# Prompt rows as a fifth tile of the compression pairs, gates evacuated in place, spatial steps spread over the pairs

## The reference, cut to what matters

```python
h = rmsnorm(x, lw['norm_g'])
proj = h @ lw['w_in']                       # q, k_cmp, v_cmp, k_sel, ..., za, u, v, zb, r
...
def compress(rows, params):                 # windows of 32 rows, one every 16
    w1, b1, w2, b2 = params
    ...
    blocks = rows[:, idx].transpose(0, 1, 3, 2, 4).reshape(B, n_cmp, G, CMP_BLOCK * dh)
    return jax.nn.gelu(blocks @ w1 + b1) @ w2 + b2
...
    kc = compress(jnp.concatenate([gather_pages(ck_cmp), k_cmp], axis=1), lw['cmp_k'])   # decode, 63 windows
    kc = compress(k_cmp, lw['cmp_k'])                                                    # prompt, 31 windows
...
v_n = layernorm(jax.nn.gelu(v), lw['v_norm_g'], lw['v_norm_b'])
sgu = jax.nn.gelu(u) * spatial_gate(v_n, lw['w_spatial'], lw['b_spatial'])
pb = (sgu * jax.nn.silu(zb)) @ lw['w_pb']
```

## Time and profile before

| | us |
|---|---|
| median of 3 runs | 543.88 |
| lowest and highest | 541.86, 543.99 |
| the profiled execution, its own time | 543.01 |
| its span in the trace | 541.3 |
| PE busy | 523.7 (97%) |
| DVE busy | 331.2 (61%) |
| ACT busy | 243.1 (45%) |
| POOL busy | 157.0 (29%) |

### The profile page before, as it was taken

One profiled execution on the slowest core, in us unless ns is written; L12 is line 12 of the kernel. 1 busy time (PEld: TensorE's weight loads), 2 busy tenths in 40 slices (PEclk: granted clock), 3 DMA queues, 4 the chain that ended last, 5 costly groups with the idle time before them and its releaser, 6 DMA issues.

```text
span 541.3 us, 12831 instructions
## 1 busy us (share of the span) xinstructions
PE 523.7 (97%) x5198; PEld 473.3 (87%) x5198; DVE 331.2 (61%) x838; ACT 243.1 (45%) x564; POOL 157.0 (29%) x257
## 2 busy tenths in 40 slices
PE   6899999999999999999989999999999999999995
PEld 4899999999999998987978766767779999999995
DVE  4723231388898765674564678687753477763565
ACT  6543424534533323241241887677674432323334
POOL 0006933044414633734000066473453000000000
PEclk9999999999999999999999999999999999999998
DMA  8527652448525465877331267563454435306104
GB/s 296 214 82 218 235 181 80 154 141 290 173 61 195 142 198 168 264 282 238 101 97 40 79 155 186 148 155 100 128 140 125 131 114 155 119 1 196 40 7 161
DMA packets 59789, 81.05 MB, mean 150 GB/s; under 512 B 7825, under 2 KB 49233, under 8 KB 59218
## 3 DMA queue, kind: packets, MB, share of 16 engines
q1 hardware_dynamic: 48320, 49.97, 30.4%
q0 software_dynamic: 10688, 29.14, 17.6%
q10 hardware_dynamic: 722, 1.12, 0.6%
HBM read 65.23 MB, written 8.13 MB: 136 GB/s over the span
## 4 chain that ended last, share of the span: by engine, by line
PE 91%; DVE 3%; issue 2%; ACT 1%; DMA 1%; POOL 1%; DVEq 0%
PE m L1729 62%; PE so L2028 4%; PE so L2037 3%; PE so L1900 3%; PE so L1903 3%; PE so L1901 3%; PE m L1813 2%; PE so L1939 2%; PE so L1877 1%; PE so L1988 1%; DMA U<-p_turn 1%; PE t L1865 1%; POOL U L1002 1%; PE t L1755 1%; PE so L1742 1%
## 5 line engine op out<-in xcount | busy, mean ns | idle before, releaser
L1729 PE MATMUL m<-h_hi,w_hi 128*128 128x272 f32 x448 | 132.7, 296 | 1.0 <-DVE za L1426 0.8
L1729 PE MATMUL m<-h_hi,w_lo 128*128 128x272 f32 x448 | 129.2, 288 | 0.0
L1729 PE MATMUL m<-h_lo,w_hi 128*128 128x272 f32 x448 | 128.7, 287 | 0.0
L1729 PE MATMUL m<-w_hi,h_hi 128*128 128x256 f32 (+2 forms) x360 | 104.1, 289 | 2.4 <-issue 1.9
L1729 PE MATMUL m<-w_hi,h_lo 128*128 128x256 f32 (+2 forms) x360 | 101.9, 283 | 0.0
L1729 PE MATMUL m<-w_lo,h_hi 128*128 128x256 f32 (+2 forms) x360 | 101.9, 283 | 0.0
L1313 DVE TENSOR_TENSOR w_lo<-raw,w_hi 128x1024 fp32r<-128x1024 f32 (+2 forms) x62 | 71.0, 1155 | 42.6 <-ACT w_hi L1046 42.5
L1729 PEld LDWEIGHTS m<-h_hi,w_hi 128*128 128x128 f32 x448 | 84.3, 188 | 13.4 <-issue 10.2
L1002 POOL DMA_DIRECT2D U<-p_turn x108 | 58.2, 547 | 104.0 <-DVE p_turn L1635 102.6
L1729 PEld LDWEIGHTS m<-h_hi,w_lo 128*128 128x128 f32 x448 | 84.5, 189 | 0.0
L1729 PEld LDWEIGHTS m<-h_lo,w_hi 128*128 128x128 f32 x448 | 84.4, 188 | 0.0
(11 more groups left out here) (301 smaller groups left out, 904.3 us busy)
## 6 DMA issues: line engine op xcount, KB each, us to landing
raw<-in_w_in SPq DMA_DIRECT2D x36, 512.0 KB
U<-in_x_p SPq DMA_DIRECT2D x8, 512.0 KB, 5.9
raw<-in_w_o SPq DMA_DIRECT2D x8, 512.0 KB
U<-p_turn POOLq DMA_DIRECT2D x54, 64.0 KB, 2.6
U<-p_turn SPq DMA_DIRECT2D x42, 64.0 KB, 2.8
raw<-in_w_in SPq DMA_DIRECT2D x8, 256.0 KB
raw<-in_w_pa SPq DMA_DIRECT2D x8, 256.0 KB
raw<-in_w_pb SPq DMA_DIRECT2D x4, 512.0 KB
```

The costliest lines, as they stand in the source:

```text
L1729: ins = mm(out, lhs(a, k), rhs(b, k), start=(k == 0 and a + b == 0), stop=(k == n - 1 and a == 1))
```

## The change

- The `hid` steps are gone. The prompt's turned rows are a fifth tile of pairs 1 and 6: five casts, five subtractions, and `hidh` and `hidl` of these two pairs have 320 columns in place of 256. The prompt's windows thereby take the split in three passes too. Its gelu is a second ScalarE instruction into `hid_rows`, and its `kc` matmuls stand among those of the pair.
- `xt_sb` grows to 5 tiles, and the second half of `w1_hi` moves to the columns that hold `kT`. `kT` is therefore written to DRAM at step `kTs` (`k_dram`, 512 KB), read back at step `kt 0 6`, and the prompt's first scores wait for it (`k_back`).
- The order: pair 1 starts one V block earlier, two V blocks stand between the pairs instead, all four turns of a pair stand ahead of what was between them, and the spatial steps stand with pair 6 (one), pair 7 (two) and pair 8 (two).
- All four U0 gates go straight into `sg` (`DIRECT`), so that two `mix` steps fall away, and a spatial step multiplies two groups into the gates.
- The squares of the decode rows are summed on VectorE with `tensor_tensor_reduce`.

```diff
-    u0 = [("main", SLOT["U0"], 1, hf) for hf in range(2)]
     u1 = [("main", SLOT["U1"], a, hf) for a in range(2) for hf in range(2)]
-    extra = {3: [("ln", NT), ("lnr",)], 6: [("sp", 2), ("sp", 3), ("ln2", 4)],
-             7: [("sp", 4), ("mix", u0[0]), ("mix", u0[1])], 8: [("mix", u1[0]), ("mix", u1[1])], 9: [("mix", u1[2])]}
+    norm = {4: 0, 6: 2, 7: 3, 8: 4}
+    extra = {3: [("ln", NT), ("lnr",)], 6: [("sp", 0)], 7: [("sp", 1), ("sp", 2)], 8: [("sp", 3), ("sp", 4)],
+             9: [("mix", x) for x in u1[:3]]}
...
+    def early(count):
+
+        n = len(order)
+        main(count)
+        order[n:] = [x for x in order[n:] if x not in (("ln", NT), ("lnr",))]
...
     order += [("w1hi", 0)]
     turn(5)
-    main(3)
-    order += [("hid", 0), ("w1lo", 0)]
+    main(2)
+    order += [("w1lo", 0)]
     for c in range(1, NCH):
         behind = [("hidl", c - 1)] if c - 1 in PAIRS else []
+        tiles = ([(c - 1, 0)] if c in WIDE_PAIRS else []) + [(c, n) for n in range(4)]
         if c == 5:
             order += behind
             turn(1)
-            order += [("sp", 0), ("w1hi", 1), ("ln2", 1), ("w1lo", 1)] + four("xh", 6) + [("hid", 5), ("kc", 4), ("sp", 1), ("ln2", 2)]
+            order += [("w1hi", 1), ("ln2", 1), ("w1lo", 1)] + [("xh", x, n) for x, n in [(5, 0)] + [(6, n) for n in range(4)]]
+            order += [("kc", 4)]
             main(1)
             continue
-        cast = four("xh", c) if c != 6 else []
+        cast = [("xh", *x) for x in tiles] if c != 6 else []
         order += cast[:2] + behind + cast[2:]
-        if c == 1:
-            main(1)
-        if c == 8:
-            order.append(u1[0])
+        if c in (2, 3):
+            early(1)
         s, after = take()
-        order += [("part", s, 0, KD)] + four("xl", c) + [("kc", c - 1), ("hidh", c)]
+        order += [("part", s, 0, KD)] + [("xl", *x) for x in tiles] + ([("kc", c - 1)] if c - 1 in PAIRS else []) + [("hidh", c)]
         turn(2)
-        if c in (4, 6):
-            order.append(("ln2", 0 if c == 4 else 3))
-        order += ([s] if c != 7 else []) + [x for x in after if x not in (("ln", NT), ("lnr",))] + extra.get(c, [])
+        if c in norm:
+            order.append(("ln2", norm[c]))
         turn(2)
+        order += [s] + after + extra.get(c, [])
     order += [("hidl", NCH - 1)]
...
-DIRECT = [("main", SLOT["U0"], 0, hf) for hf in range(2)]
+DIRECT = [("main", SLOT["U0"], a, hf) for a in range(2) for hf in range(2)]
...
-        w1_hi = [placed("w1_hi0", 3072, [P, 8, P], F32R), placed("w1_hi1", 5376 + 4104, [P, 8, P], F32R)]
+        w1_hi = [placed(f"w1_hi{n}", 3072 - 1024 * n, [P, 8, P], F32R) for n in range(2)]
         w1_lo = placed("w1_lo", 5376 + 11272, [P, 16, P], F32R)
-        xt_sb = placed("xt_sb", 5376, [P, 4100], F32R)
-        xt_hi, xt_lo = xt_sb[:, 0:2050], xt_sb[:, 2050:4100]
+        xt_sb = placed("xt_sb", 5376, [P, 5124], F32R)
+        xt_hi, xt_lo = xt_sb[:, 0:2562], xt_sb[:, 2562:5124]
...
+                elif s[0] == "kTs":
+                    for y in range(2):
+                        wait_evacuated(sp, T_AT[("kT", y)])
+                    sp.dma_start(k_dram, kT[:, :, :]).then_inc(k_saved, 16)
+                elif s == ("kt", 0, 6):
+                    sp.wait_ge(hid_sum, len(PAIRS))
+                    sp.dma_start(kT[:, :, :], k_dram).then_inc(k_back, 16)
...
-                    _, before, m = TURNS[t - RING]
-                    if before in PAIRS:
-                        pool.wait_ge(xt_lo_done, 4 * PAIRS.index(before) + m + 1)
-                    else:
-                        pool.wait_ge(hid_sum, before + 1)
+                    pool.wait_ge(xt_lo_done, LOW_AT[TURNS[t - RING][1:]] + 1)
...
+                    if i == NT:
+                        continue
...
-                        if s == DIRECT[0]:
-                            act.wait_ge(hid_sum, 1)
-                        nc.scalar.activation(sg[:, 0, s[3] * HALF:(s[3] + 1) * HALF], m[:, 0:HALF], ACT.Gelu_apprx_tanh).then_inc(main_act, 1)
+                        nc.scalar.activation(sg[:, s[2], s[3] * HALF:(s[3] + 1) * HALF], m[:, 0:HALF], ACT.Gelu_apprx_tanh).then_inc(main_act, 1)
...
+                        act.wait_ge(k_saved, 16)
...
+                    if c in WIDE_PAIRS:
+                        x = S[k % 2][:, 0:320].rearrange("p (g n) -> p g n", g=G)
+                        nc.scalar.activation(out, x[:, :, 0:P], ACT.Gelu_apprx_tanh, bias=b1)
+                        nc.scalar.activation(hid_rows.rearrange("p (g n) -> p g n", g=G)[:, :, 0:NCP], x[:, :, P:P + NCP],
+                                             ACT.Gelu_apprx_tanh, bias=b1).then_inc(hid_ready, 1)
+                    else:
+                        nc.scalar.activation(hid_at[k % 2], S[k % 2][:, 0:256], ACT.Gelu_apprx_tanh, bias=b1).then_inc(hid_ready, 1)
...
+                elif kind == "sq" and s[1] == NT:
+                    x = x_in[0:TS, NT, :]
+                    dve.wait_ge(x_loaded[NT], 16)
+                    v.tensor_tensor_reduce(U[0:TS, 10240:11264], x, x, 1.0, 0.0, ALU.mult, ALU.add, st[0:TS, NT:NT + 1]).then_inc(rows_squared, 1)
...
-                        dve.wait_ge(hid_sum, 1)
                         dve.wait_ge(kc_ready, 4)
                         for s0 in DIRECT:
                             wait_main_read(dve, s0)
                     else:
                         wait_evacuated(dve, T_AT[("sp", i - 1)])
-                        dve.wait_ge(kc_ready, 5)
                     if i < NT:
-                        v.tensor_tensor(sg[:, 1:4, tok(i)], tb[:, P:4 * P].rearrange("p (g n) -> p g n", g=3),
-                                        b_sp[:, P:4 * P].rearrange("p (g n) -> p g n", g=3), ALU.add)
-                        seq(v.tensor_tensor(sp_t[:, 0:r], tb[:, 0:r], b_sp[:, 0:r], ALU.add))
+                        t4, b4 = (x.rearrange("p (g n) -> p g n", g=4) for x in (tb[:, :], b_sp))
+                        v.tensor_tensor(sg[:, 2:4, tok(i)], t4[:, 2:4, :], b4[:, 2:4, :], ALU.add)
+                        seq(v.tensor_tensor(sp_t[:, :, :], t4[:, 0:2, :], b4[:, 0:2, :], ALU.add))
...
-                elif kind == "hid":
-                    c = s[1]
-                    k = TURN_AT[c, 0]
-                    pe.wait_ge(w1_loaded[c // 5], 16)
-                    pe.wait_ge(x_turned, k + 1)
-                    if c >= 2:
-                        pe.wait_ge(hid_ready, c - 1)
-                    x = ring[:, k % RING, :].rearrange("p (r g e m) -> p r e g m", r=4, g=G, e=2)
-                    for j in range(16):
-                        o, r, e = j // 8, j // 2 % 4, j % 2
-                        ins = mm(S[c % 2][:, 0:2 * NCP], w1_at[c // 5][:, j, :], x[:, r, e, :, o:o + NCP], start=(j == 0), stop=(j == 15))
-                    ins.then_inc(hid_sum, 1)
...
-                            return part[:, 512 * r + o:512 * r + o + 512].rearrange("p (g e n) -> p e g n", g=G, e=2)[:, e, :, :]
+                            return part[:, 640 * r + o:640 * r + o + 640].rearrange("p (g e n) -> p e g n", g=G, e=2)[:, e, :, 0:n]
...
+                            mm(out, w, x(xt_hi), start=(j == 0), stop=False, skip_group_check=True)
+                            ins = mm(out, w1_lo[:, j, :], x(xt_hi), start=False, stop=False, skip_group_check=True)
                         else:
-                            ins = mm(out[:, 0:256], w, x(xt_lo), start=False, stop=(j == 15), skip_group_check=True)
+                            ins = mm(out, w, x(xt_lo), start=False, stop=(j == 15), skip_group_check=True)
```

More of the change, by code:

```diff
@@ L154 @@
 PAIRS = [c for c in range(NCH) if c % 5]
+PAIR = {c: n for n, c in enumerate(PAIRS)}
+PAIR.update({c: PAIR[c + 1] for c in range(0, NCH, 5)})
+WIDE_PAIRS = [c + 1 for c in range(0, NCH, 5)]
 TILES = (3, 2, 1, 0)
@@ L468 @@
 TURN_AT = {s[1:]: n for n, s in enumerate(TURNS)}
+HIGH_AT = {s[1:]: n for n, s in enumerate(x for x in ORDER if x[0] == "xh")}
+LOW_AT = {s[1:]: n for n, s in enumerate(x for x in ORDER if x[0] == "xl")}
 NKEY = 3 * QB
@@ L993, in _ @@
                     load_upto(TURN_AT[s[1:]] + RING + 1)
[L994 to L998 removed]
+                elif s == ("sp", NT):
+                    wait_evacuated(pool, T_AT[s])
+                    pool.wait_ge(out_done, 16 * N_OUT)
+                    for k in range(7):
+                        load_key(0, k)
                 elif s[0] == "tt" and moves_with(s[1]) == s[1]:
@@ L2021, in _ @@
                         pe.wait_ge(s_exp, NQ)
+                        pe.wait_ge(k_back, 16)
                     for c in range(2):
```

137 lines of the change are left out of this document (67 added, 70 removed).

## The result

| | us |
|---|---|
| kernel before, median of 20 runs | 542.53 |
| kernel after, median of 20 runs | 544.03 |
| ratio after to before, 95% interval | 1.0025 (1.0013 to 1.0037) |
| profiled execution of after, its span | 544.36, 542.6 |

The change made the kernel a quarter of a per cent slower: by the medians 1.5 us, clear of noise but small. I had forecast 2.8 us faster, 540.6, with a range from 538.0 to 543.2; 544.03 lies outside it. The first part of the page (busy us, share, instructions) shows what was meant to happen: TensorE has 64 matmuls fewer than in the earlier trace rows and is busy 1.5 us less. The span is 1.3 us longer all the same.

What follows compares the result with a forecast made beforehand. TensorE, busy 97% of the span, was taken to bound the kernel; -4.2 us of matmuls, +2.2 of stalls and -0.8 at the start gave -2.8, so 540.6 us, range 538.0 to 543.2.

Steps and rivals of the forecast that it cites:

- start: Kernel start: with the decode rows' squares on VectorE, TensorE goes on sooner; -0.8 us, bounds 0 and -0.9.
- (a): Before the first `hidh`, where `hid` stood: TensorE waits for five casts on ScalarE; +0.45 us.
- the two `hid`: The two `hid` steps in the compression are removed from TensorE; -7.1 us.
- wide passes: Pairs 1 and 6: 96 matmuls grow from 256 to 320 columns; +2.9 us.
- prompt's `kc`: The prompt's `kc` matmuls only move into pairs 1 and 6; taken as 0.
- (b): `kc` of pair 4, directly behind `hidl`, waits for ScalarE's gelu; +0.8 us.
- (c): `hidh` of pair 4 waits for a late load, turn, `ln`, `lnr` and casts; +1.0 us, 0 to 3.0 by landing time.
- (d): Pair 7: copies of pair 8 meet its loads, so its casts come late; +0.2 us, 0 to 1.5.
- old stall of 0.23: The 0.23 us in which TensorE idles in the compression before the change goes away.
- My signs of being wrong: Landings of over 6 us in more than one pair, or wide matmuls at 0.13 us.
- "no gain": Rival: VectorE waits for landings in several pairs, (c) and (d) come to 4.5 us; 543.6 us, chance 0.20.
- "slower" rival: A circle of subtraction, load and turn closes from landings of 5.2 us, seven pairs lose 1.5 each; about 549.8, chance 0.05.

Runs made afterwards that it cites:

- experiment 11: Kernel of experiment 9 with the two wide passes back at 256 columns, so the compressed prompt rows are not computed: 535.15 us (0.9852).
- experiment 13: Changed kernel with its order kept, only SyncE's 16 window copies moved out of the compression to an earlier stretch: 539.84 us (0.9942).
- experiment 1: Changed kernel with the decode rows' statistics and square root (`ln`, `lnr`) moved ahead of the last two turns of pair 4: 539.03 us (0.993).
- Experiments 3: Changed kernel with 20 useless matmuls of 128x256 filling TensorE's wait before `kc` 3: 542.67 us (1.0002).
- experiment 14: The changed kernel as it is, run again beside its filled version: 544.71 us (1.0024).
- 15: Changed kernel with 20 useless matmuls in the wait before `kc` 3, run again beside experiment 14: 542.89 us (0.9992).
- experiment 7: Kernel before with only the squares of the decode rows moved to VectorE: 541.79 us (0.9977).
- experiments 4: Changed kernel with the squares of the decode rows back on ScalarE: 544.36 us (1.0026).
- 12: Kernel before with only SyncE's 16 window copies moved out of the compression to an earlier stretch: 542.14 us (0.9988).
- 5: Kernel of experiment 1 with `kc` 4 put behind one more block of U0: 540.55 us (0.9944).
- experiment 2: Changed kernel with four window copies issued by SyncE at other pairs, the four of 117.4 us moved to 160.8: 542.29 us (0.9985).
- 8: Kernel of experiment 1 with `kc` 4 covered and the first pair's first two casts ahead of the last V block's evacuation: 540.53 us (0.9939).
- 10: The same edit as experiment 1, run again beside later kernels: 539.93 us (0.9942).
- 9: Kernel of experiment 8 with SyncE's 16 window copies moved out of the compression to an earlier stretch: 537.93 us (0.9904).

## Why the prediction was wrong

The table goes term by term, on the two profiled executions. Measured are TensorE's steps from start to next start, so a wait counts with the 0.07 to 0.15 us in which the last matmul before it runs out.

| term | predicted | measured |
|---|---|---|
| start | -0.8 | -0.27 |
| (a) first `hidh` | +0.45 | +0.50 |
| the two `hid` | -7.1 | -7.1 |
| wide passes | +2.9 | +2.5 (by experiment 11: 2.8) |
| prompt's `kc` | 0 | +0.4 |
| (b) `kc` 4 | +0.8 | +0.77 |
| (c) `kc` 3 and `hidh` 4, waits | +1.0 | +3.43 |
| (c) the low clock behind them | not in the sum | +1.47 |
| (d) pair 7 | +0.2 | 0 |
| old stall of 0.23 | -0.23 | -0.23 |
| all other steps | 0 | -0.2 |
| sum | -2.8 | +1.3 |

The sum on the right is the difference of the spans, 542.6 - 541.3, and it arrived at the end whole, as I had said. (The forecast in us also stood on a kernel before of 543.4, from three runs; its median over 20 is 542.53. In the direction of the change, -2.8 was forecast and +1.5 measured.)

**The step that failed is (c).** Its mechanism was right: all four turns ahead of the `ln` of the decode rows, `lnr` behind it, the casts behind that. The gelu of `kc` 3 stands in the same chain, so most of the wait shows before `kc` 3 and not, as I had expected, before `hidh` 4. Taken as a price, (c) was 1.0 and came to 3.43, and its sizes were wrong in two places. First the landing: I took 4.7 us, because "SP has four copies near this place", between 6.7 and 3.3; it was 5.90, 1.2 more. Nothing in the rows spoke for the middle: by my own line, 6.7 us gave a stall of 3.0. Second the issue: I put the fourth load at the start of `hidh` 3 (132.67), and it was issued at 133.47, 0.8 later. VectorE, which had waited 1.1 us for a load of pair 3 and had been busy since, came a few tenths late to the `ln` of V; the rest is in the steps from the first subtraction to the two issues, which took longer than the 0.6 and 1.3 us that I had. The last 0.4 is my rounding from 1.2 down to 1.0, and small steps. In experiment 13 VectorE has its loads after 3.9 and 3.6 us; what remains is 0.57 us of waiting before `hidh` 4 and a block ahead of `kc` 3 that lasts 3.27 us in place of some 3.1, so there (c) is less than the 1.0 that I took.

Either remedy alone takes the loss away: the order in experiment 1, the copies in experiment 13, each about 5 us. So the loss needs both, the late load and the chain behind it.

**What the sum left out is the clock.** Behind the wait of 2.68 us and that of 0.57 the clock fell to its lower level, and the next `hidh` lost 1.5 us more. Experiments 3, 14 and 15 show it, in two series. Nothing in the trace of before told it, since TensorE never stops for more than 0.23 us in the compression, and behind the 1.86 us at the start it kept the clock.

**The start** gave 0.44 (from 2.90 to 2.46 between the end of TensorE's first block and its next one), and 0.17 of that went since the first block took longer. In the thirteen other profiles with the squares on VectorE the same stretch is 2.04 to 2.29 us, thus 0.6 to 0.9 less than 2.90, and experiment 7 agrees by time.

**My signs of being wrong.** One of the two came true: landings of over 6 us in more than one pair. In the changed kernel the last load of pair 3 was issued at 119.30 and turned at 125.72 (6.4 us), the third of pair 4 took 6.3, and the third of pair 7, issued at 162.45, was turned at 169.03 (6.6). Each had window copies issued within 2.5 us ahead of it. VectorE waited in six turns for key loads, 7.5 us in all, and in two for value loads of pair 7, 3.1 us; but in this profile only pair 4 passed its wait on to TensorE; there the square root, the table load and the casts stood behind it. (In that of experiment 14 TensorE also waited 0.61 us for the `w_lo` that follows the turns of pair 3.) The wide matmuls came 0.15 us apart, as forecast for a `hidh` of 4.8 to 4.9 us (4.84 and 4.76).

**The rivals.** The time of "no gain" (543.6) was the nearest, and its mechanism, waits for landings, was the right one, though it wanted them to reach TensorE in several pairs. The circle of the "slower" rival did not close, though it was to do so from landings of 5.2 us: the late landings of pairs 3 and 7 reached TensorE nowhere, and in pair 2 a load took 3.9 us (106.87 to 110.80). The terms (a), (b), `hid` and the wide passes held; the prompt's `kc`, which I took as nothing, cost 0.4 us.

The expected gain is thus there. Take `ln` and `lnr` back in front of the last two turns, and the kernel is 3.6 us (539.03 against 542.62) and 2.6 us (539.93 against 542.57) under the kernel before, where the forecast said 2.8. With the copies out of the way as well and the two small waits covered it is 4.6 us under it, at 537.93.

## What to carry to other kernels

When a change puts a chain (statistics, square root, table load, casts) behind a transfer, price it with the latest landing that the trace shows near other traffic, and not with a value between: what decides is which step stands behind the transfer in its engine's order, and moving one step by two places was worth 5 us here. Look at what other queues send just ahead of a load that someone waits for, and at the traffic without a deadline first. A wait of TensorE can cost, besides its own length, a stretch at half clock behind it (1.5 us lost here); the runs give no length of wait below which it is safe.

## What the runs showed of the hardware

- The granted clock after a wait. Behind 3.25 us of waiting, in two parts (2.68 and 0.57), the matmuls ran at 1.2 GHz for some 3.4 us (0.21 apart, then 0.12); filling the longer part with matmuls kept 2.4 GHz. How long the wait is does not decide alone. The clock also fell behind 1.84 and 1.86 us (experiments 4 and 12) and behind 0.99 us with 0.32 us shortly before it (5). It stayed at 1.00 behind 1.86 us (the kernel before), 2.23 + 0.57 (4), 1.38 (2, before `hidh` 7) and 0.99 (8). What else decides stays open.
- Indirect loads of 256 KB, from the start of the issue to the start of the turn that waited for them, took 3.6 to 4.0 us in experiment 13, which has no window copies near them. With four copies of 254 KB begun up to 3.7 us ahead they took 5.9 to 8.0 (the changed kernel, experiments 1, 5 and 10), with the copies just behind 5.0 (experiment 1). In experiment 2, with the copies begun 3.9 us ahead, it was 4.7.
- 64 columns more in a stream of 128x256 matmuls cost 2.8 us for 96 matmuls (experiment 11 against 9), 0.029 us each, which is one column in 0.45 ns; by the steps of the two profiles it is 2.5 us.
